# Decoder block on one core: conditioning sums moved to VectorE rows, first stage run chunk by chunk

## What is computed

```python
c_act = silu(c)                                   # 1024 numbers
mod = c_act @ w_ada[l] + b_ada[l]                 # 1024 x 9216: nine sections of 1024
sh1, sc1, gt1, sh2, sc2, gt2, sh3, sc3, gt3 = split(mod, 9)
h = rmsnorm(x, g_ffn1) * (1 + sc1) + sh1
x = x + 0.5 * gt1 * swiglu(h, ffn1_w1, ffn1_w3, ffn1_w2)
h = rmsnorm(x, g_mix) * (1 + sc2) + sh2
x = x + gt2 * hybrid_mixer(h, ...)
h = rmsnorm(x, g_ffn2) * (1 + sc3) + sh3
x = x + 0.5 * gt3 * swiglu(h, ffn2_w1, ffn2_w3, ffn2_w2)
shf, scf = split(c_act @ w_ada_final + b_ada_final, 2)
out = rmsnorm(x, g_final) * (1 + scf) + shf
```

## Time and profile before

| quantity | value |
|---|---|
| median of 3 runs | 1863.17 us (1862.52 to 1863.54) |
| the profiled execution, its own time | 1860.78 us |
| its span, first to last instruction | 1859.0 us |
| PE busy | 1810.6 us, 97% of the span, 8370 matmuls |
| DVE busy | 1261.2 us, 68% |
| ACT busy | 774.6 us, 42% |
| PE, share of the chain that ended last | 86% |
| DVE, share of that chain | 8% |

### The profile page before, as it was taken

The page is one execution under the profiler, slowest core; times in us unless marked ns, Lnnn a source line. Parts: engine busy times, 40 slices in busy tenths (PEclk is TensorE's granted clock), DMA queues, the critical chain, the costliest instruction groups (busy, mean ns, idle before and its releaser), DMA issues.

```text
span 1859.0 us, 23169 instructions
## 1 busy us (share of the span) xinstructions
PE 1810.6 (97%) x8370; PEld 1472.2 (79%) x8370; DVE 1261.2 (68%) x1951; ACT 774.6 (42%) x1393; POOL 268.3 (14%) x411
## 2 busy tenths in 40 slices
PE   6999999999999999999999999999999999999997
PEld 3778888888888887888877777778888888888886
DVE  5887777777576786444326668787667666576767
ACT  5643333333344565211125666663333333344445
POOL 2011211211210000000303330201111111111000
PEclk9999999999999999999999999999999999999998
DMA  8165565665765321111211110424545545476432
GB/s 324 58 235 205 200 231 193 225 216 181 266 215 155 106 69 70 56 34 57 68 38 42 46 35 1 176 97 159 196 170 181 207 153 193 159 261 215 125 97 91
DMA packets 100529, 269.77 MB, mean 145 GB/s; under 512 B 13120, under 2 KB 13504, under 8 KB 100288
## 3 DMA queue, kind: packets, MB, share of 16 engines
q1 hardware_dynamic: 65680, 150.50, 24.0%
q0 software_dynamic: 34304, 117.46, 18.5%
q10 hardware_dynamic: 432, 0.34, 0.1%
HBM read 209.53 MB, written 54.53 MB: 142 GB/s over the span
## 4 chain that ended last, share of the span: by engine, by line
PE 86%; DVE 8%; ACT 3%; issue 1%; DMA 1%; POOL 0%; ACTq 0%; DVEq 0%; POOLq 0%
PE PS L1554 62%; PE PS L1550 23%; DVE Wl L1021 1%; DVE NMax L1463 1%; PE PS L1988 1%; DMA AdaFirst<-ada 1%; DVE X L1359 1%; DVE X L1122 1%; ACT X L701 0%; ACT Bh L701 0%; DVE CT L1428 0%; DVE Bl L1128 0%; DVE SqSum L1328 0%; DVE Ml L1262 0%; DVE TmpA L1346 0%
## 5 line engine op out<-in xcount | busy, mean ns | idle before, releaser
L1554 PE MATMUL PS<-Bh,Wh 128*128 128x512 f32 x1120 | 437.5, 391 | 4.5 <-ACT T L684 4.1
L1554 PE MATMUL PS<-Bh,Wl 128*128 128x512 f32 x1120 | 435.9, 389 | 0.0
L1554 PE MATMUL PS<-Bl,Wh 128*128 128x512 f32 x1120 | 435.8, 389 | 0.0
L1554 PEld LDWEIGHTS PS<-Bh,Wh 128*128 128x128 f32 x1120 | 210.3, 188 | 50.7 <-DVE Wl L1021 4.9
L1554 PEld LDWEIGHTS PS<-Bh,Wl 128*128 128x128 f32 x1120 | 210.2, 188 | 44.0
L1554 PEld LDWEIGHTS PS<-Bl,Wh 128*128 128x128 f32 x1120 | 210.3, 188 | 43.1
L1554 PE MATMUL PS<-Wh 128*128 128x512 f32 x616 | 240.0, 390 | 0.0
L1554 PE MATMUL PS<-Wh,Wl 128*128 128x512 f32 x616 | 239.7, 389 | 0.0
L1554 PE MATMUL PS<-Wl,Wh 128*128 128x512 f32 x616 | 239.7, 389 | 0.0
L1053 DVE TENSOR_TENSOR Wl<-RawB,Wh 128x512 fp32r<-128x512 f32 x154 | 106.5, 692 | 130.3 <-ACT Wh L659 129.3
L659 ACT ACTIVATE Wh<-RawB 128x512 fp32r<-128x512 f32 x154 | 97.3, 632 | 230.7 <-PE PS L1554 230.7
(11 more groups left out here) (201 smaller groups left out, 2872.6 us busy)
## 6 DMA issues: line engine op xcount, KB each, us to landing
Raw<-up_w SPq DMA_DIRECT2D x86, 512.0 KB, 5.3
Ada<-ada POOLq DMA_DIRECT2D x72, 512.0 KB, 4.3
g_dram<-T SPq DMA_DIRECT2D x88, 256.0 KB, 2.3
W2s<-down_w POOLq DMA_DIRECT2D x88, 256.0 KB, 4.5
s_dram<-W2s POOLq DMA_DIRECT2D x88, 256.0 KB, 2.8
GQ<-g_dram POOLq DMA_DIRECT2D x88, 256.0 KB, 3.4
RawB<-s_dram SPq DMA_DIRECT2D x88, 256.0 KB, 2.9
RawB<-down_w SPq DMA_DIRECT2D x66, 256.0 KB, 2.7
```

Source lines behind the costliest of these rows:

```text
L1554: return nc.tensor.matmul(out, lhs, rhs, start=first, stop=last, skip_group_check=True)
```

## The change

**Later sections.** The matrix arrives turned around: a tile now holds 128 of the section's outputs as partitions and all 1024 inputs along the row. `ada_tile` is one DVE instruction that multiplies the tile with `CRow` (silu of `c`, the same in all partitions) and writes the sum along the row into one column of `Mod`. `ada_cols`, `ada_between`, `second_cols` and `AdaSum` are gone. `CRow` is loaded once in each up stage (512 KB, SP, behind the plain group), and ACT takes its silu at t = 11; the first `ada_tile` waits for that.

**The start.** SC1 and the second half of SH1 are made in the same way, one tile for each chunk k (`row_tile`), followed by a scale for that chunk alone (`row_scale`). Only the first half of SH1 stays on PE (8 row products, 4 columns). The loads are reordered: `CRow0` and half 0 of `x`, the small SH1 block, half 1 of `x`, then one tile (k < 4) or two (k > 3) for each chunk. `copy_r` (ACT) copies the spread inverse norm from PSUM to `RS`.

**The order of the plain group.** In the first FFN the chunks run k by k, both halves of a chunk together. The second FFN keeps its order.

```diff
+        def chunk_at(ph, c):
+            return divmod(c, KT) if ph else (c % NH, c // NH)
...
@@ SP
-                for q in (0, 2, 1, 3):
+                for q in (0, 2):
+                    spill(ph, 0, q)
+                sp.wait_ge(prod, N_FFN * ph + 8)
+                sp.wait_ge(bcast_done, 2 + 4 * ph)
+                sp.dma_start(CRow[:], ada[SECTIONS * KT]).then_inc(row_loaded, 16)
+                for q in (1, 3):
                     spill(ph, 0, q)
...
+            sp.dma_start(CRow0[:], ada[SECTIONS * KT]).then_inc(row_loaded, 16)
+            for c in (0, 2):
+                load_x_first(sp, 0, c)
+            sp.wait_ge(x_loaded[6], 16)
...
@@ POOL
+            def load_tile(section, k):
+                if k == KT - 1:
+                    pool.wait_ge(ada_used, 2)
+                pool.dma_start(row_part(section, k), ada[section * KT + k]).then_inc(second_loaded[k], 16)
...
@@ ACT
+                    if ph == 0 and c == 0:
+                        copy_r(1)
+                        for o in (2, 3):
                             prep_hi(0, o)
...
+                    if t == 11:
+                        act.wait_ge(row_loaded, 16 * (ph + 2))
+                        nc.scalar.activation(CRow[:], CRow[:], ACT.Silu).then_inc(c_act, 1)
...
             for k in range(KT):
                 square_first(0, k)
+            root(0)
+            copy_r(0)
             for k in range(KT):
                 square_first(1, k)
...
@@ DVE
-                nc.vector.tensor_tensor(X[:, h, k, :], X[:, h, k, :], PS[:, 7 - h, :], ALU.mult).then_inc(nm_done, 1)
+                nc.vector.tensor_tensor(X[:, h, k, :], X[:, h, k, :], PS[:, 7 - h, :] if ph else RS[:, h, :], ALU.mult)\
+                    .then_inc(nm_done, 1)
...
+                if ph == 0:
+                    t_add(ph, 0, 1)
                 plain_mul(ph, 0)
                 plain_mul(ph, 2)
-                t_add(ph, 0, 1)
+                if ph:
+                    t_add(ph, 0, 1)
...
             def ada_tile(s, k):
+                if s in (ADA_IN[0][0], ADA_IN[1][0]) and k == 0:
+                    dve.wait_ge(c_act, 3 if s == ADA_IN[0][0] else 4)
                 dve.wait_ge(ada_loaded[n % 2], 16 * (n // 2 + 1))
-                if k == 0:
-                    dve.wait_ge(cols_done, s + 1)
-                    nc.vector.tensor_scalar(AdaSum[:], Ada[:, n % 2, :], CAct[:, 0:1], None, ALU.mult).then_inc(ada_used, 1)
-                else:
-                    dve.wait_ge(ada_used, s * KT + k)
-                    nc.vector.scalar_tensor_tensor(AdaSum[:], Ada[:, n % 2, :], CAct[:, k:k + 1], AdaSum[:],
-                                                   ALU.mult, ALU.add).then_inc(ada_used, 1)
+                a = s * KT + k
+                nc.vector.scalar_tensor_tensor(Ada[:, n % 2, :], Ada[:, n % 2, :], 1.0, CRow[:], ALU.mult, ALU.mult,
+                                               accum_out=Mod[:, a:a + 1]).then_inc(ada_used, 1)
+            def row_tile(section, k):
+                a, tile = section * KT + k, row_part(section, k)
+                dve.wait_ge(second_loaded[k], 16 if k < KH else 32)
+                nc.vector.scalar_tensor_tensor(tile, tile, 1.0, CRow0[:], ALU.mult, ALU.mult,
+                                               accum_out=Mod[:, a:a + 1]).then_inc(ada_used, 1)
...
@@ PE
-            def ada_between(ph, t):
-                for y in range(KT - 1, KT * len(ADA_IN[ph]), KT):
-                    if ada_step(ph, y) + 2 == t:
-                        if y == KT - 1:
-                            pe.wait_ge(silu_done, silu_no(ph, 0, 3))
-                        ada_cols(ADA_IN[ph][y // KT])
...
-            def ada_cols(s, bank=7):
-                pe.wait_ge(ada_used, (s + 1) * KT)
-                for c in range(KT):
-                    made = mm(PS[:, bank, c:c + 1], AdaSum[:, blk(c)], Ones[:], True, True)
-                made.then_inc(cols_done, 1)
```

More of the change, by code:

```diff
@@ L142 @@
 NCOLS = _at
+NM_FIRST = ((0, 0), (0, 1), (1, 0), (1, 1), (0, 2), (0, 3), (1, 2), (1, 3))
 MEANS, BCASTS = ((4, 6, 9), (3, 6, 9)), ((5, 7, 10), (4, 7, 10))
@@ L189, in program @@
         Ada, _ = place("Ada", [P, 2, D], like=z_at)
-        AdaSum, _ = place("AdaSum", [P, D], like=z_at + 8 * K)
+        CRow, _ = place("CRow", [P, D], like=z_at + 8 * K)
         W2s, _ = place("W2s", [P, 4, HALF], like=tmp_at)
@@ L289, in scores, with row_part, chunk_no, nm_no @@
             return flat(PS[:, 2 * c:2 * c + 2, :])[:, first * P:last * P]
+        def row_part(section, k):
+            second = 1 if section == SH1 else 0
+            if k == 6:
+                return AdaLate[:, second, :]
+            return AdaTile[:, k if k < KH else second if k == KT - 1 else 2 * k - KH + second, :]
+        def chunk_at(ph, c):
+            return divmod(c, KT) if ph else (c % NH, c // NH)
+        def chunk_no(ph, h, k):
+            return h * KT + k if ph else NH * k + h
+        def nm_no(ph, h, k):
+            if ph:
+                return NH * KT + h * KT + k + 1
+            return NM_FIRST.index((h, k)) + 1 if k < KH else NH * k + h + 1
         def operand(h, k):
@@ L847, in _ @@
                 square_first(0, k)
+            root(0)
+            copy_r(0)
             for k in range(KT):
                 square_first(1, k)
-                if k == 1:
-                    root(0)
+            act.wait_ge(row_used, KT)
+            nc.scalar.activation(AdaRow[0:1, :], PS[0:1, 0, :], ACT.Copy).then_inc(row_done, 1)
+            for o in (0, 1):
+                prep_hi(0, o)
             root(1)
[L853 to L857, removed]
             up(0)
@@ new lines, in plain_group @@
+            def plain_group(ph):
+                for c in range(NH * KT):
+                    h, k = chunk_at(ph, c)
+                    if ph and h == 0 and k == 1:
+                        mean(5)
+                    elif ph and h == 0 and k == 4:
+                        bcast(5)
+                    pe.wait_ge(b_lo, 24 * ph + c + 1)
+                    which, kk = operand(h, k)
+                    for j in range(4):
+                        o = 4 * (k // KH) + j
+                        bank = PLAIN_BANKS[h][j]
+                        if h == 0 and k % KH == 0:
+                            pe.wait_ge(w_lo, N_FFN * ph + o + 1)
+                        if k == 0:
+                            plain_free(ph, h, j)
+                        w = blk(k % KH)
+                        mm(PS[:, bank, :], Wh[:, o, w], Bh[which][:, kk, :], k == 0, False)
+                        mm(PS[:, bank, :], Wh[:, o, w], Bl[which][:, kk, :], False, False)
+                        made = mm(PS[:, bank, :], Wl[:, o, w], Bh[which][:, kk, :], False, k == KT - 1)
+                        if k == KT - 1:
+                            made.then_inc(prod, 1)
+                        elif h == 1 and k == KH - 1 and j == 3:
+                            made.then_inc(half_used, 1)
```

263 lines of the change are left out of this document (121 added, 142 removed).

## The result

The changed kernel takes 1845.05 us (median of 4 runs, 1844.79 to 1845.72), against 1863.16 us for the kernel before beside it (1862.52 to 1863.54). The ratio is 0.9904, with a 95% interval of 0.9887 to 0.9921: 18.1 us less, where 18.9 were forecast. The profiled execution took 1845.72 us itself (its span 1843.9).

What follows compares the result with a forecast made beforehand. PE was taken as the bound behind the first 108 us. Blocks -16.2, start -3.5 and clock +0.8 made -18.9 us: 1860.78 becomes 1841.9, or 1844.3 us with 2.4 added for the median; range 1838 to 1854.

Steps and rivals of the forecast that it cites:

- clock term: Half clock on PE after longer pauses before tiles 8 and 12: 0.8 us added, ends 0 and 2.4.
- The nine blocks: Column sums between PE's tiles behind 100 us go: 9 x 1.80 = 16.2 us gained, all on the path.
- a gain that turns into waits: Rival: PE only just ahead of DVE in the up stage, so the 16.2 us return: 1860, no change; 3%.
- The sum along the row: DVE's multiply with sum: 1.19 us plus 0.1 for the read (0 to 0.27); in the up stage nothing on the path.
- half rate: Rival: DVE's sums take 2.38 instead of 1.19 us, 11 times in the start: 13.1 us, giving 1857.4; 5%.
- a dear sum: Rival, slower: 2.05 us more on each of DVE's 11 row tiles uses up the gain; 2.4 more gives 1881; 3%.
- The start, 3.5 us: Start gains 3.5 us at tile 12, though PE begins 11.7 us sooner; from 7 us gained to 3 us lost.
- the head: First step of the start, to the lo part of the first chunk on DVE: ends at 31.5 us.
- the walk: Timing of the start step by step along DVE's queue, which was taken to decide tile 12.
- The body: Start, from first to sixteenth chunk's lo part on DVE: 39.5 us, ending at 71.0 against 73.2 before.
- The tail: Start, from the sixteenth chunk's lo part to the first tile's weights on DVE: 10.4 us, 11.7 before.
- The early beginning is kept whole: Rival: tile 8 starts behind a shorter plain group and all 11.7 us of PE's earlier beginning count: 1835; 5%.

Runs made afterwards that it cites:

- `later_only`: Kernel before with only the later sections changed (multiplies with a row sum, `CRow`, no column sums on PE); start as before: 1845.90 us.
- `start_only`: Changed kernel with the later sections' edit undone and the column sums put back on PE, so only the start is changed: 1862.04 us.
- `head_sooner`: Changed kernel with the root of half 1 ahead of the first two weight splits on ACT, and SP's first weight loads released sooner: 1843.70 us.
- `pe_plus`: Changed kernel with ten more unused 128-column products on PE just before the first plain group: 1845.96 us.
- `before_again`: The kernel before, unedited, run and traced a second time: 1862.65 us.
- `after_again`: The changed kernel, unedited, run and traced again: 1844.46 us.
- `after_evict`: Changed kernel with five evictions (tiles 8, 9, 10 on ACT; 11, 12 on DVE) moved to where their tile has just ended: 1840.39 us.

## Why the prediction was right, and where it was not

The time, 1845.05, is 0.7 us from the forecast of 1844.3 and well in the range. The mechanism that was to carry it did. The start was wrong: with its clock term it was forecast at -2.7 us and brought -0.9 by medians. The blocks brought 0.8 us more than forecast, and that the sum still came out within a microsecond is in part luck.

*The nine blocks.* Right: 16.2 us forecast, 1.83 us a block measured, 16.5 in all; `later_only` has 17.0 by medians. The half microsecond more stays open; in the traces 0.8 us of the gain lie between the two up stages, which the change doesn't touch. No wait took the blocks' place; the windows show PE full at full clock. The rival of a gain that turns into waits is out.

*The sum along the row.* I had put 0 to 0.27 us for the read and took 0.1; it is 0. The rivals of half rate and of a dear sum are out: 1.14 us from start to start, 72 times. By the Trainium skill, "Vector Engine (DVE) Microarchitecture Reference", section 7, it should have run at half the throughput. With the 1.19 us of the earlier trace rows that would be an estimated 2.38 us, and the trace doesn't agree: here the measurement decides, and with the sum this shape takes no longer than a multiply-add without one.

*The start, 3.5 us.* This is the term that was mis-sized: tile 12 came 0.4 to 0.7 us later in these traces, and `start_only` gained 0.9 us by medians. By its steps: the head took 2.2 us longer. The mean began at 27.81, near the 27.7 of the walk, but from there to the end of DVE's copy of the inverse root (31.92) it took 4.1 instead of 2.0 us, since I left out that the root stands behind a weight split on ACT that waits 3.16 us for its load; `head_sooner` gave it back. I had walked ACT's squares there, but not its weight splits. The body took 40.8 instead of 39.5 us: DVE's own work was right (36.1 busy, 36.6 forecast), its waits were 4.5 instead of 2.9. The tail took 11.2 instead of 10.4: of the 0.8 us more, `plain_mul` waits 0.47 for PE's chunks and the next lo part 0.20 for ACT. PE began at 34.98 instead of 31.5, at half clock (0.50 from 31 to 36 us), and ended its group at 80.5 instead of 76 us. `pe_plus` shows that this coupling is real. With the five evictions moved the whole start is worth 1.3 us.

*The clock and the median.* I added 0.8 us for a drop behind tile 12, and 2.4 us to go from the profiled execution to the median. `before_again` shows a drop of 2.1 us that the execution first traced had not, and lacks the one at the end that this had. If most executions of before have both, which their times fit but no trace shows, the drop behind tile 12 is in the median of before already and nearly cancels between medians; I had counted it as new. The terms by medians are -17.0 and -0.9 instead of -16.2 and -3.5 + 0.8.

*The early beginning is kept whole.* Out: that rival's 1835 is 10 us under the measured time. But the wait at tile 12, which I took as DVE's stream, was in part a matter of order in the queues of ACT and DVE: `after_evict` moved nothing but evictions and gained 4.5 us.

## What to carry to other kernels

Work taken from a full engine in its full stage is worth its start-to-start time, and can be counted from one trace. An earlier beginning is worth only what gets through the last wait before that stage: follow that wait back through the in-order queue of the engine that ends it, since what stands ahead there (a load not landed, a sum of another engine) may be moved away for more than the beginning brings. Then look where the next wait comes up. And trace the same kernel twice before a trace is set against a median: here two traces of one program differed by 2 us in a single stage.

## What was not expected of the hardware

A DVE multiply with a sum along 1024 columns, both inputs float32 in SBUF, took 1.14 us from start to start, and the read of its accumulator (0.08 us long) delayed nothing. PE's clock was granted at half, 1.2 GHz, behind the pause of 6.46 us before tile 8 and behind every pause of 3.7 to 3.9 us at tile 12 that was traced, for a stretch that differed between executions of one program (behind tile 12 some 6.8 us in the first trace of the changed kernel and 3.4 us in `after_again`, worked out from the windows between 104.5 and 112 us); behind the pauses of 2.53 and 2.57 us it stayed at full. The two traces with these short pauses had an early drop that delayed PE where it would wait anyway, and `before_again`, without that, had the late drop that costs 2.1 us. No run forces either drop, so that the one spares the other is a reading of three traces and not shown.
